# First norm's factors as spread rows, tiles transposed inside the first products, constants of the next layer loaded in the last product

## The reference

```python
x = layer_norm(x, ln0_g, ln0_b)                      # the first norm
for i in range(2):
    h = x @ w_in[i]                                  # 1024 -> 1536: q, k, v of two attentions
    oa = global_axial_attention(...)                 # rms norm of q and k with gains, rope, softmax
    ob = window_sink_attention(...)                  # rope, band mask, sink
    mix = concat(rms_norm(oa, ...), rms_norm(ob, ...)) @ w_out[i]
    x = layer_norm(ALPHA * x + mix, ln1_g[i], ln1_b[i])
    g, v = split(x @ w_up[i]); g = conv3(g) + conv_b[i]
    ffn = (gelu(g) * v) @ w_down[i]                  # 2816 -> 1024, the last product of a layer
    gate = sigmoid(x @ w_ple_gate[i] + b_ple_gate[i])
    x = layer_norm(ALPHA * x + ffn + gate * (p[i] @ w_ple[i]), ln2_g[i], ln2_b[i])
```

## Time and profile before

| | us |
|---|---|
| median of 3 runs (lowest to highest) | 1215.49 (1215.14 to 1216.63) |
| time of the profiled execution | 1215.36 |
| its span from first to last instruction | 1213.6 |
| PE (TensorE matmul) busy in the span | 1192.3 |
| POOL (GpSimd) busy | 593.9 |
| DVE (VectorE) busy | 526.7 |
| ACT (ScalarE) busy | 492.4 |
| mean granted TensorE clock, share of full | 0.997 |

### The profile page before, as it was taken

The page is one execution under the profiler, slowest core; times in us unless marked ns, Lnnn a source line. Parts: engine busy times, 40 slices in busy tenths (PEclk is TensorE's granted clock), DMA queues, the critical chain, the costliest instruction groups (busy, mean ns, idle before and its releaser), DMA issues.

```text
span 1213.6 us, 17810 instructions
## 1 busy us (share of the span) xinstructions
PE 1192.3 (98%) x5800; PEld 974.2 (80%) x5800; DVE 526.7 (43%) x1098; ACT 492.4 (41%) x899; POOL 593.9 (49%) x342
## 2 busy tenths in 40 slices
PE   7999999999999999999999999999999999999997
PEld 6887778888888888888878777788888888888886
DVE  7777847532122134211477777375211122431108
ACT  3456753344344333323144767433443333332321
POOL 6665844455443444344155756634653444434442
PEclk9999999999999999999999999999999999999999
DMA  6321213344333332222132202433433333222331
GB/s 220 88 74 49 88 45 113 113 130 139 98 92 87 103 104 95 79 97 95 56 90 70 80 27 70 126 116 89 139 104 104 100 90 102 90 85 91 102 104 70
DMA packets 122854, 115.68 MB, mean 95 GB/s; under 512 B 6816, under 2 KB 97952, under 8 KB 122784
## 3 DMA queue, kind: packets, MB, share of 16 engines
q1 hardware_dynamic: 122784, 114.81, 30.7%
HBM read 112.70 MB, written 2.10 MB: 95 GB/s over the span
## 4 chain that ended last, share of the span: by engine, by line
PE 93%; DVE 2%; DVEq 1%; issue 1%; POOL 1%; DMA 1%; ACT 0%; SPq 0%; ACTq 0%
PE ps L1219 28%; PE ps L1221 28%; PE ps L1220 28%; PE ps L1371 3%; PE ps L1385 3%; PE ps L1359 1%; PE ps L1361 1%; PE ps L1342 1%; PE ps L1229 1%; POOL w_lo L537 1%; DMA scratch<-in_ln_b_dram 1%; DVEq L875 0%; DVEq L1202 0%; DVE x L880 0%; POOL ln_r L533 0%
## 5 line engine op out<-in xcount | busy, mean ns | idle before, releaser
L527 POOL TENSOR_TENSOR w_lo<-raw,w_hi 128x1024 fp32r<-128x1024 f32 x192 | 461.7, 2406 | 411.4 <-ACT w_hi L635 411.4
L1219 PE MATMUL ps<-xt_hi,w_hi 128*128 128x512 f32 x704 | 273.9, 389 | 0.0
L1220 PE MATMUL ps<-xt_lo,w_hi 128*128 128x512 f32 x704 | 273.9, 389 | 0.0
L1221 PE MATMUL ps<-xt_hi,w_lo 128*128 128x512 f32 x704 | 273.9, 389 | 0.0
L635 ACT ACTIVATE w_hi<-raw 128x1024 fp32r<-128x1024 f32 x192 | 201.9, 1055 | 132.7 <-PE ps L1221 66.6
L1219 PE MATMUL ps<-w_hi,stat 128*128 128x512 f32 x480 | 188.3, 392 | 0.0
L1220 PE MATMUL ps<-w_lo,stat 128*128 128x512 f32 x480 | 187.1, 390 | 0.0
L1221 PE MATMUL ps<-w_hi,stat 128*128 128x512 f32 x480 | 187.0, 390 | 0.0
L1219 PEld LDWEIGHTS ps<-xt_hi,w_hi 128*128 128x128 f32 x704 | 132.1, 188 | 27.6
L1220 PEld LDWEIGHTS ps<-xt_lo,w_hi 128*128 128x128 f32 x704 | 132.1, 188 | 27.5
L1221 PEld LDWEIGHTS ps<-xt_hi,w_lo 128*128 128x128 f32 x704 | 132.1, 188 | 27.3
(11 more groups left out here) (123 smaller groups left out, 1330.8 us busy)
## 6 DMA issues: line engine op xcount, KB each, us to landing
raw<-in_w_up_dram SPq DMA_DIRECT2D x88, 512.0 KB, 3.8
raw<-in_w_down_dram SPq DMA_DIRECT2D x44, 512.0 KB, 3.2
raw<-in_w_in_dram SPq DMA_DIRECT2D x26, 512.0 KB, 3.8
raw<-in_w_out_dram SPq DMA_DIRECT2D x16, 512.0 KB, 3.8
raw<-in_w_ple_gate_dram SPq DMA_DIRECT2D x16, 512.0 KB, 3.9
scratch<-in_ln_g_dram SPq DMA_DIRECT2D x5, 512.0 KB, 4.5
scratch<-in_ln_b_dram SPq DMA_DIRECT2D x5, 512.0 KB, 6.0
raw<-in_w_ple_dram SPq DMA_DIRECT2D x4, 512.0 KB, 3.7
```

The costliest lines, as they stand in the source:

```text
L527: pool.tensor_tensor(w_lo[:, n, :], raw[:, n % RAW, :], w_hi[:, n, :].bitcast(F32), ALU.subtract).then_inc(w_split.sem, 1)
L1219: pe.matmul(out, a[0], b[0], start=first, stop=False)
L1220: pe.matmul(out, a[0], b[1], start=False, stop=False)
L1221: return pe.matmul(out, a[1], b[0], start=False, stop=last)
```

## The change

The gain and bias of the first norm are loaded as two rows of 4 KB, into one partition. TensorE spreads each over 128 partitions with matmuls by a row of ones, into PSUM banks 6, 7 (gain) and 2, 3 (bias). VectorE centres tile t in place and scales it in place, reading the factor from PSUM. First weight tile and tile 1 of x move forward in SP's order.

Only tile 0 is transposed before the layers. Tiles 1, 2, 3 are transposed between the halves of steps 0, 1, 2, in both layers; the second transposition of the last product ("norm2", 1) goes away. ScalarE runs `norm_hi(n + 1)` behind `body_hi(4 + n)` and ahead of the squares. On VectorE `norm_lo(1)` stands between statistics and centring of tile 2 in the first layer, and behind the last norm at the end of a layer; `norm_lo(2)` stands behind `rotate` of step 0, `norm_lo(3)` behind `rotate` of step 1.

The rope tables are made once before the layers, and for the next layer ahead of the norms of the last product; SP loads the constants once before the layers and then among the last weight tiles of the last product. In attention "rot" moves from g = 6, 10, 14, 18 to 7, 11, 15, 19, the second "p_t" from 26 to 27, and on VectorE `mean_squares` moves ahead of `qkt_lo`.

```diff
-WARM = (8, 9)
+WARM = (2, 3, 4)
@@ pe_plan
         steps.append(("win", c, t, 0))
+        if n < 3:
+            steps.append(("norm_in", n + 1))
+        elif n == 3:
+            steps.append(("rot", 0, 1))
+        steps.append(("win", c, t, 1))
+        if n < 2:
+            continue
         if n == 2:
             steps.append(("rot", 0, 0))
-        steps.append(("win", c, t, 1))
-        if n < 2:
-            steps.append(("norm_in", n + 2))
...
-        if g in (6, 10, 14, 18):
-            steps.append(("rot", 2, (g - 6) // 4))
-        if g in (25, 26):
-            steps.append(("p_t", g - 25))
+        if g in (7, 11, 15, 19):
+            steps.append(("rot", 2, (g - 7) // 4))
+        if g in (25, 27):
+            steps.append(("p_t", (g - 25) // 2))
@@ SP
             load_x(0)
-            sp.dma_start(ln_g, bcast(ln0_g)).then_inc(first_gain_landed.sem, 16)
-            sp.dma_start(ln_b, bcast(ln0_b)).then_inc(norm_landed.sem, 16)
-            load_x(1)
+            for i, v in enumerate((ln0_g, ln0_b)):
+                sp.dma_start(rows[:, i, :, :], v.rearrange("(o a n) -> o a n", o=1, a=2)).then_inc(rows_landed.sem, 16)
...
             first_load(0)
+            load_x(1)
             first_load(1)
@@ GpSimd
+            pool.memset(masks[:, :, :], 0.0)
+            pool.memset(ones_row, 1.0)
+            pool.drain().then_inc(warm_made.sem, 1)
...
             ln_root(0, 1)
-            ln_root(1, 2)
             first_lo(0)
             first_lo(1)
-            ln_root(2, 3)
+            ln_root(1, 2)
             first_lo(2)
             first_lo(3)
+            ln_root(2, 3)
             ln_root(3, 4)
@@ ScalarE
             first_hi(0)
+            first_hi(1)
             norm_hi(0, 1)
-            first_hi(1)
             first_hi(2)
-            norm_hi(1, 3)
             first_hi(3)
...
                         body_hi(4 + n)
+                        if n < 3:
+                            norm_hi(n + 1, tr_full.at(layer, TR["norm_in", n + 1] + 1))
+                        if n == 3:
+                            qkt_evac(0, 1)
+                        win(c, t)
...
+            norm_hi(1, tr_full.at(DEPTH, TR["norm_in", 1] + 1))
@@ VectorE
             for t in range(TT):
                 dve.wait_ge(x_landed[t].sem, 16)
                 norm_stats(t, x[:, t, :])
...
                 if t in (1, 2):
                     norm_lo(t - 1, 2 * t - 1)
+                gain, bias = (ps[:, b:b + 2, :].rearrange("p a n -> p (a n)") for b in (6, 2))
+                if t == 0:
+                    dve.wait_ge(rows_spread.sem, 2)
+                dve.scalar_tensor_tensor(out=x[:, t, :], in0=x[:, t, :], scalar=mv[:, t, 0:1], in1=gain, op0=ALU.subtract,
+                                         op1=ALU.mult)
+                dve.drain()
+                dve.wait_ge(ln_rstd.sem, t + 1)
+                if t == 0:
+                    dve.wait_ge(rows_spread.sem, 4)
+                dve.scalar_tensor_tensor(out=x[:, t, :], in0=x[:, t, :], scalar=ln_r[:, t:t + 1], in1=bias, op0=ALU.mult,
+                                         op1=ALU.add).then_inc(ln_done.sem, 1)
...
             dve.wait_ge(fixed_landed.sem, 16)
+            gain_tables(64)
...
-                norm_lo(2, xt_hi_done.at(layer, 1))
...
                         rotate(c, t)
-                        if n == 0:
-                            norm_lo(3, xt_hi_done.at(layer, 3))
+                        if n < 2:
+                            norm_lo(n + 2, xt_hi_done.at(layer, 3 + 2 * n))
...
+                gain_tables(const_landed.at(layer, 128))
                 for t in range(TT - 1):
                     wait_down(dve, layer, t)
                     norm_sum(t, DOWN_BANK[t], ln_rstd.at(layer, 4 + t + 1), norm_landed.at(layer, 64), down_free)
-                    if t in (1, 2):
-                        norm_lo(t - 1, xt_hi_done.at(layer, 13 + 2 * (t - 1)))
+                    if t == 1:
+                        norm_lo(0, xt_hi_done.at(layer, 15))
...
+                norm_lo(1, xt_hi_done.at(layer, 17))
@@ TensorE
+            pe.wait_ge(warm_made.sem, 1)
+            keep_warm(WARM[0])
+            pe.wait_ge(rows_landed.sem, 32)
+            for i, bank in enumerate((6, 2)):
+                for n in range(2):
+                    pe.matmul(ps[:, bank + n, :], ones_row, rows[:, i, n, :], start=True, stop=True).then_inc(rows_spread.sem, 1)
+            keep_warm(WARM[1])
             pe.wait_ge(const_made.sem, 1)
-            keep_warm(WARM[0])
-            for t in range(2):
...
+            for _ in norm_t(0, 1):
+                pass
+            keep_warm(WARM[2])
```

More of the change, by code:

```diff
@@ L117, in transposes_of @@
     use, n = {}, 0
-    for s in steps + [("norm2", 0), ("norm2", 1)]:
+    for s in steps + [("norm2", 0)]:
         if s[0] in ("rot", "probs_t", "sumsq", "p_t"):
@@ L431, in _, with load_constants @@
             sp.dma_start(rope_sb[:, :, :, :], rope).then_inc(fixed_landed.sem, 16)
-            with sp.Fori(0, DEPTH) as layer:
-                def raw_free(s):
-                    sp.wait_ge(w_split.sem, w_split.at(layer, s - AHEAD - RAW + 1))
-                sp.wait_ge(h_done.sem, h_done.at(layer, 0))
+            def load_constants(layer):
                 sp.dma_start(cols[:, :], columns[bass.ds(layer, 1)].rearrange("a p n -> (a p) n")).then_inc(const_landed.sem, 16)
@@ L442, in _, with raw_free @@
                 sp.dma_start(sinks[:, :], bcast(sink[bass.ds(layer, 1)].rearrange("a n -> (a n)"))).then_inc(const_landed.sem, 16)
+            load_constants(0)
+            with sp.Fori(0, DEPTH) as layer:
+                def raw_free(s):
+                    sp.wait_ge(w_split.sem, w_split.at(layer, s - AHEAD - RAW + 1))
                 for s in range(AHEAD, UP_AT):
@@ L481, in _ @@
                         load(s, down_source(layer, i * 2 + v), 1)
+                following = (layer + 1) % DEPTH
+                sp.wait_ge(h_done.sem, h_done.at(layer, FT))
+                load_constants(following)
                 for r in range(1, REST):
@@ L670, in win @@
                     if c == 0:
-                        act.wait_ge(ln_done.sem, ln_done.at(layer, 0))
+                        act.wait_ge(down_free.sem, down_free.at(layer, 0))
                         if n >= 2:
@@ L852, in _ @@
                 norm_hi(0, tr_full.at(layer, TR["norm2", 0] + 1))
-                norm_hi(1, tr_full.at(layer, TR["norm2", 1] + 1))
                 body_hi(STREAM + 2)
                 body_hi(STREAM + 3)
+            norm_hi(1, tr_full.at(DEPTH, TR["norm_in", 1] + 1))
         @block.vector
@@ L1122, in _ @@
                         n = c * TT + t
-                        if n == 2:
-                            qkt_lo(0, 0)
+                        if n == 3:
+                            qkt_lo(0, 1)
                         if n == 2 * TT - 1:
@@ L1136, in _ @@
                         qkt_lo(1, 3)
-                    if g in (7, 11, 15, 19):
-                        qkt_lo(2, (g - 7) // 4)
+                    if g in (15, 23, 31):
+                        mean_squares((g - 15) // 8)
+                    if g in (8, 12, 16, 20):
+                        qkt_lo(2, (g - 8) // 4)
                     if 0 < g <= GROUPS:
@@ L1159, in _ @@
                 outb(1)
-                norm_lo(0, xt_hi_done.at(layer, 5))
+                norm_lo(0, xt_hi_done.at(layer, 7))
                 outb(2)
-                norm_lo(1, xt_hi_done.at(layer, 7))
+                norm_lo(1, xt_hi_done.at(layer, 9))
                 outb(3)
-                norm_lo(2, xt_hi_done.at(layer, 9))
+                norm_lo(2, xt_hi_done.at(layer, 11))
                 for q in range(2 * TT):
@@ L1167, in _ @@
                     if q == 0:
-                        norm_lo(3, xt_hi_done.at(layer, 11))
+                        norm_lo(3, xt_hi_done.at(layer, 13))
                     gate_apply(*divmod(q, TT))
@@ L1461, in _ @@
                         if n == 0:
-                            pe.wait_ge(xt_split.sem, xt_split.at(layer, 4 + 2 * t + 2))
+                            pe.wait_ge(xt_split.sem, xt_split.at(layer, 6 + 2 * t + 2))
                         if i < 2:
@@ L1485, in up_tile @@
                         ins.then_inc(w_used.sem, 1)
-                pe.wait_ge(xt_split.sem, xt_split.at(layer, 12))
+                pe.wait_ge(xt_split.sem, xt_split.at(layer, 14))
                 pe.sem_inc(ffn_begun.sem, 1)
@@ L1525, in _ @@
                         signal(ins, down_full, r == REST - 1, t)
-                    if t in (1, 2):
-                        if t == 1:
-                            pe.wait_ge(down_free.sem, down_free.at(layer, 1))
-                        body_norm_t(t - 1, ("norm2", t - 1), ln_done.at(layer, 4 + t))
+                    if t == 1:
+                        pe.wait_ge(down_free.sem, down_free.at(layer, 1))
+                        body_norm_t(0, ("norm2", 0), ln_done.at(layer, 5))
                 for n in range(2):
@@ L1536, in _ @@
```

(2 more changed lines are left out.)

90 lines of the change are left out of this document (37 added, 53 removed).

## The result

The change makes the kernel slightly slower. In interleaved runs on one chip the kernel before took 1216.32 us (median of 20 runs, 1214.80 to 1216.85) and the changed one 1218.00 us (median of 20, 1217.27 to 1218.79): ratio 1.0015, 95% interval 1.0009 to 1.0021. The profiled executions, 1215.36 before and 1218.03 after, lie 2.7 apart, their spans 2.6 apart (1213.6 and 1216.2). The medians lie only 1.7 apart because the runs of the kernel before gather at two values, near 1215.2 and near 1216.7, and its profile is of the lower. The explanation goes by the spans. The forecast was 1214.2, the range 1210.3 to 1217.8: missed, and with the wrong sign.

The account below looks back on a forecast made before the run. TensorE was taken as the bound, busy 1192.3 of 1213.6 us. Start +4.8, attention -3.2 and -1.8, second layer's begin +0.2, end -1.2: total -1.2 from 1215.36, forecast 1214.2, range 1210.3 to 1217.8.

Parts of the forecast that it names:

- Start, third low part: Start, GpSimd: low parts of weight tiles 0, 1, 2 done, w_split at 3, at 15.0 (14.5 to 16.4).
- the spreading: Start, TensorE: four float32 matmuls of 512 columns take 2.2 at 2.4 GHz, 4.3 at 1.2; no cost on the path.
- T: Start: the moment w_split reaches 3, releasing the load of weight tile 4; forecast 15.0.
- From T to step 2: Start: 6.85 until VectorE's norm_lo(1), then 14.2 of its queue; step 2 at 36.1 against 33.76, +2.3.
- Transposes of tile 3: Start, TensorE: transposes now behind step 2's start, 0.79 and a slow restart, +0.9.
- The clock: Start: TensorE's stand before step 2 brings the 1.2 GHz level, +1.6 (0 to 2.6).
- Attention: Both layers: waits at the second p_t and first low part go, -3.2; sumsq and rot no longer meet, -1.8.
- The term at "rot" and "sumsq": Attention: the two no longer meet at g = 14, saving 0.44 and 0.45 a layer, -1.8.
- Second layer's begin: Steps 1 and 2 of layer two: a wait of 1.7 replaces one of 2.1; sum +0.2 (-0.5 to +1.5).
- End: Last layer: norm_lo(1) leaves VectorE's queue ahead of the last tile, -1.2.
- The third: Rival, start: slower, w_split reaches 3 late, at 19.8, 4.8 later; time 1219; chance 0.10.
- The fourth rival: Attention: moved transposes change nothing, waits reappear at g = 15 and 27; 5.0 of gain missing, 1219.2; chance 0.04.

Follow-up runs that it names:

- the first experiment: Only the moves inside attention (rot, second p_t, mean_squares ahead of qkt_lo), on the kernel before: 1208.88 us, ratio 0.994.
- the stand filled: Both edits plus 12 rounds of 8 warm matmuls in TensorE's stand ahead of step 2: 1205.89 us, ratio 0.992; once more 1206.23, ratio 0.9921.
- both edits: Changed kernel with spreading matmuls in four row groups and norm_hi(n + 1) ahead of body_hi(4 + n): 1207.51 us, ratio 0.9934; once more 1209.19, ratio 0.9946.

## Why the prediction was wrong

**Start, third low part: the step that failed.** The prediction took 15.0 for the moment at which `w_split` reaches 3; it was 19.7. The prediction priced the spreading at 2.2 to 4.3 from the earlier trace rows and wrote "Cost on the path: none, since `w_hi(0)` and GpSimd's low parts cover it. Without that cover it would cost up to 2." Both sentences fell. The price was 7.2. The earlier trace rows was the wrong neighbour: those matmuls fill 64 columns of the array, and their eight instructions follow each other every 0.135 (their outputs go in turn to partitions 0 to 63 and 64 to 127; whether that is why they are quicker, no run tested). One of 128 columns of output, such as the float32 transposes of the earlier trace rows, eight in 0.79 for 128 columns of data each, takes 0.099 per 128, so 0.40 for 512 at 2.4 GHz and 0.79 at 1.2. A float32 matmul is two such instructions in the trace; eight of them are 6.3, near the 7.2 measured. The right row was on record, four groups further down. And the level was the lower one: the warm matmuls behind the spreading run at 0.11 each (24 in 2.74), the later ones at 0.055. The Trainium skill, page FP8 and Floating Point Precision, section "TensorE Precision Notes", gives true float32 as four passes through the array; at 1.2 GHz that is an estimate of 6.8 for four matmuls of 512. The trace, with 7.2, agrees with it better than with my row, which gave 4.3.

The cover was no cover, because it was entered from the wrong end: GpSimd's roots take their place between the low parts, and the second root waits for statistics that VectorE makes behind the bias. The terms of T, forecast and measured: tile 0 used 6.0 and 6.85; second low part done 12.1 and 13.2; idle for the root 0 and 1.27; idle for the third high part 0 and 2.18. The kernel with four row groups (issue at 16.16) puts 3.7 of the 4.7 on the spreading, 1.0 is left for the tiles' landing. The kernel with the third high part first confirms the second idle time by itself: 2.2. Within the 3.7 a part is the warm matmuls behind the spreading, which the prediction had at nothing too: tile 0 is scaled at 12.7 (11.44 and 1.28), and its transposes start at 14.0, when the 24 are done. An estimate from these rows is that they cost 1.0 to 1.3; no run took the warm matmuls out alone. TensorE was not warm earlier either, as the prediction had it: these eight transposes take 1.79, and 1.09 in the kernel before.

**From T to step 2: right.** Forecast 6.85 + 14.2 = 21.05. Measured 40.87 - 19.7 = 21.2, and the same 21.2 in the kernels with row groups (37.19 less 15.9) and with the third high part first (38.63 less 17.4). The stand of VectorE at `norm_lo(1)` was there (5.31), and the kernel with `norm_hi` first took it away.

**Transposes of tile 3: right**, 0.8 for 0.9. **The clock: right in kind**, 2.6 in the profiled execution for 1.6, at the top of its 0 to 2.6. The Trainium skill, TensorE: Matmul & The Clock Gate, section "HAM oscillation", has the half rate come back over an idle gap. Here the half rate was there when step 2 began in every profile of a kernel whose stand ahead of it was left empty (stands of 3.6 to 8.5 us), and where that stand was filled it was not.

**Attention: mechanism right, size low**, 3.1 to 3.3 a layer for 2.5. The term at "rot" and "sumsq" was 1.55 in place of 0.9. It had been read off the two named waits alone; the restart behind each and a small wait at an earlier "rot" came on top.

**Second layer's begin: right within its range**, -0.2 for +0.2; the wait at step 1 was 1.4 for 1.7, and one of 0.6 at step 2. With `norm_hi` first the first of them shrinks to 0.4. **End: right**, -1.3 for -1.2.

The sum of the misses: 4.8 at step 2, 0.8 at transposes and clock, -1.3 in attention, -0.4 at the second layer, -0.1 at the end: 3.8, from -1.2 to +2.6. The attention's extra 1.3 was not foreseen and hid a part of the start's miss, which is 5.6 by itself.

**The rivals.** The third had the outcome, by luck: its T of 19.8 and its time of 1219 were measured as 19.7 and 1218.0. Its cause was not: it was to be a late weight tile, and that tile was only 0.85 late. The prediction's bounds for T, 14.5 to 16.4, held only the tile and the root; the spreading had no line in them, although its own price was open by a factor of two. The fourth rival (moved transposes change nothing) is refuted by the first experiment.

The change is then three things: attention, -6.3 and good by itself; the last norms, -1.3; a new start, +10.4, of which 3.7 is the placing of four matmuls and 5.0 one queue position (the second layer's begin is the -0.2 that is left). Mended in these two places it runs 0.54 to 0.66% under the kernel before, and with the stand filled 0.8%, the best that ran. The attention's moves alone gave 1208.88 where both edits gave 1207.51 in the same job, so the mended start adds 1.4 to them, and the filled stand about as much again or more. Not tried: undoing the moved transposes of the first tiles alone.

## What to carry to other kernels

Price a new matmul by a row of the same type that fills as many columns of the array, and at the clock that the engine will have at that moment; a float32 matmul early in a kernel is dear. "Hidden" is a statement about a queue: follow who stands behind each instruction on every engine that the new result passes, down to the semaphore that releases the next load. When a wait is moved behind an in-order engine's transfer-bound work, try the other order first: here two lines swapped gave 5 us at step 2.

## What the runs showed of the hardware

Matmuls on one row each, placed on partitions 0, 32, 64 and 96, ran side by side: 2.09 for the eight instructions that took 7.19 on one row. The Trainium skill, TensorE: Matmul & The Clock Gate, section "Why this matters for your kernels", names this for small contractions and reports 3.07 times for four tiles. Here it was 3.4.

TensorE was still at its lower level when the 7.2 us of one-row matmuls ended: the warm matmuls behind them took 0.11 each, those from 15.42 on 0.055. The granted-clock column doesn't show that; a window over them reads 1.00 (changed kernel):

```profile
11.30:14.00 2.70, 2.70 (x26) 2.70 (x26) 2.49 (x4) 0.00 (x0) 1.93 (x1) 1.00 1.02 390
```

So at the head of a trace the duration of a known instruction tells the level, not the column.

A VectorE instruction with both tiles in SBUF took 3.37 beside a GpSimd low part and 1.28 alone, and GpSimd's own work grew too (5.65 for 4.78). The Trainium skill, SBUF — State Buffer, section "SBUF: two separate sides", states that exclusion. The trace agrees, and 2.1 at step 2 is its price in the kernel with factors by DMA. The term of the root that the prediction built on it (0.55 for 1.51) was measured as 0.55.
